# Past keys turned by VectorE and moved by DMA, a new order of the attention turn, and the causal mask added by a matmul

## The reference, cut to what matters

```python
z = einsum('bqhd,bkhd->bhqk', q, k) * HD_B ** -0.5 + bias      # 16 heads, 64 wide
mask = arange(Lk)[None, :] < (q_offset + arange(Lq))[:, None]
u = where(mask, log_sigmoid(-z), 0.0)
rev_excl = cumsum(u, axis=3, reverse=True) - u
A = where(mask, exp(log_sigmoid(z) + rev_excl), 0.0)
out = einsum('bhqk,bkhd->bqhd', A, v)
```

## Time and profile before

| | |
|---|---|
| median of 3 runs | 1518.87 us (1518.58 to 1518.95) |
| the profiled execution's own time | 1517.85 us |
| its span | 1516.1 us |
| attention stage, first projection slice to the last pair's end | 793.8 to 1098.9 us of the span |
| one steady turn | 35.6 us, of which PE busy 31.46, DVE 23.00, ACT 18.62 |
| DMA in the steady turn | 164 GB/s, mean busy share 0.51 |

### The profile page before, as it was taken

One profiled execution on the slowest core, in us unless ns is written; L12 is line 12 of the kernel. 1 busy time (PEld: TensorE's weight loads), 2 busy tenths in 40 slices (PEclk: granted clock), 3 DMA queues, 4 the chain that ended last, 5 costly groups with the idle time before them and its releaser, 6 DMA issues.

```text
span 1516.1 us, 33061 instructions
## 1 busy us (share of the span) xinstructions
PE 1463.3 (97%) x13048; PEld 1391.0 (92%) x13048; DVE 1140.3 (75%) x1855; ACT 776.6 (51%) x1192; POOL 320.0 (21%) x307
## 2 busy tenths in 40 slices
PE   8999999999999999999998888888899999999998
PEld 8999999989999999999997777777699999999998
DVE  7866666668998989889726666666679989899753
ACT  6544444436754636455514555554557546364543
POOL 3000000002322323223141111111243223223221
PEclk9999999999999999999999999999999999999999
DMA  5133333223787786876426554553247777877721
GB/s 189 57 87 86 86 86 86 86 87 93 154 175 166 159 182 149 170 168 147 125 84 210 169 175 162 169 167 112 72 105 153 171 170 157 172 160 163 171 84 63
DMA packets 237716, 205.83 MB, mean 136 GB/s; under 512 B 8268, under 2 KB 224404, under 8 KB 237588
## 3 DMA queue, kind: packets, MB, share of 16 engines
q1 hardware_dynamic: 151346, 147.34, 30.9%
q0 software_dynamic: 68160, 47.20, 20.0%
q10 hardware_dynamic: 18082, 9.48, 2.3%
HBM read 192.19 MB, written 11.80 MB: 135 GB/s over the span
## 4 chain that ended last, share of the span: by engine, by line
PE 88%; DVE 5%; issue 4%; ACT 2%; DVEq 0%; DMA 0%; ACTq 0%
PE acc L2771 21%; PE acc L3095 19%; PE pMO L3095 12%; PE pL L3095 12%; PE acc L3195 5%; PE acc L3032 2%; PE pL L2892 1%; PE acc L3302 1%; PE pMO L3262 1%; PE acc L3318 1%; PE pMO L2961 1%; PE acc L3483 1%; PE acc L3291 1%; DVE pg L2544 1%; PE pMO L3249 1%
## 5 line engine op out<-in xcount | busy, mean ns | idle before, releaser
L654 POOL TENSOR_TENSOR wlo<-wraw,whi 128x512 fp32r<-128x512 f32 x40 | 56.2, 1433 | 455.2 <-ACT whi L768 455.2
L2771 PE MATMUL acc<-xa_hi,whi 128*128 128x288 f32 x544 | 125.2, 311 | 0.6 <-issue 0.6
L854 ACT ACTIVATE hi<-wraw 128x1024 fp32r<-128x1024 f32 x60 | 63.7, 1062 | 106.5 <-DVE wraw L1976 106.2
L2771 PE MATMUL acc<-xa_hi,wlo 128*128 128x288 f32 x544 | 116.6, 296 | 0.0
L837 ACT ACTIVATE hi<-wraw 128x1024 fp32r<-128x1024 f32 x60 | 63.7, 1061 | 102.8 <-PE acc L3095 102.6
L2771 PE MATMUL acc<-xa_lo,whi 128*128 128x288 f32 x544 | 116.2, 295 | 0.0
L3095 PE MATMUL acc<-X_lo,hi 128*128 128x288 f32 x384 | 113.4, 295 | 0.0
L3095 PE MATMUL acc<-X_hi,lo 128*128 128x288 f32 x384 | 113.4, 295 | 0.0
L3095 PE MATMUL acc<-X_hi,hi 128*128 128x288 f32 x384 | 113.2, 295 | 0.0
L1991 DVE TENSOR_TENSOR lo<-wraw,hi 128x1024 fp32r<-128x1024 f32 x60 | 73.4, 1223 | 41.9 <-ACT hi L837 41.9
L3095 PE MATMUL acc<-H_hi,hi 128*128 128x288 f32 x336 | 99.4, 296 | 1.3 <-DVE lo L1997 1.3
(11 more groups left out here) (513 smaller groups left out, 4943.8 us busy)
## 6 DMA issues: line engine op xcount, KB each, us to landing
wraw<-in_w_up_dram SPq DMA_DIRECT2D x64, 512.0 KB, 6.8
wraw<-in_w_down_dram SPq DMA_DIRECT2D x64, 512.0 KB, 6.2
Kp<-in_cache_k_dram SPq DMA_DIRECT2D x32, 512.0 KB, 4.0
Vp<-in_cache_v_dram SPq DMA_DIRECT2D x32, 512.0 KB, 5.6
wraw<-in_w_in_a_dram SPq DMA_DIRECT2D x30, 512.0 KB, 5.1
wraw<-in_w_up_dram POOLq DMA_DIRECT2D x32, 256.0 KB, 4.9
S_even<-in_w_up_dram POOLq DMA_DIRECT2D x32, 256.0 KB, 7.0
S_odd<-in_w_up_dram POOLq DMA_DIRECT2D x32, 256.0 KB, 8.1
```

The costliest lines, as they stand in the source:

```text
L654: ins = pool.tensor_tensor(wlo[s][:, k:k + 2, :], wraw[s][:, k:k + 2, :], whi[s][:, k:k + 2, :].bitcast(F32), ALU.subtract)
L854: act.activation(blocks4(hi31), by_depth(G % 2)[:, 0], ACT.Copy).then_inc(piece_hi, 1)
L2771: last = pe.matmul(acc[a][:, hf, 0:HALF], w[s][:, k, a * P:(a + 1) * P], x[k][:, hf * HALF:(hf + 1) * HALF], start=(k == 0 and n == 0), st ...
```

## The change

- **Keys.** `t_fill` and both `t_copy` are gone. A new `keys_turned(s, g)` on VectorE turns one page (128x1024) within 32x32 blocks into a new buffer `KX`, which holds two pages. A new `keys_moved(s, h)` on SP brings the blocks to their places in `KT` with 16 DMAs per half, each from 32 partitions to 32 partitions, 2 KB a partition. `key_page(s, g)` now waits for `keys_turned` of the page that had the buffer. The turning runs one sequence further ahead (j+2 in turn j).
- **Mask.** `mask` is gone. `logits` has two more matmuls for each query block, identity by mask matrix, both held as float32r, in the same PSUM accumulation; `gates` waits for `z_full`.
- **Banks.** `values_transposed` writes to `TB`; `weights_transposed` alternates between `pM` and `TB`; `new_sums` and `new_values` use `pO`; `fg` shrinks to one group.
- **Order.** All streams have a new order in the turn; SP's loop is written out.

```diff
+            def keys_moved(s, h):
+
+                sp.wait_ge(k_turned, 4 * s + 2 * h + 2)
+                wait(sp, zS_full, 2 * s + h)
+                for a in range(4):
+                    for b in range(4):
+                        sp.dma_start(KT[32 * b:32 * b + 32, a], KX[32 * a:32 * a + 32, b]).then_inc(k_moved, 16)
             def pages_and_weights(j, weights, more_pages):
-                kv_store(j)
-                key_page(j + 1, 2)
-                key_page(j + 1, 3)
-                value_pages(j + 1)
                 if more_pages:
                     key_page(j + 2, 0)
                     key_page(j + 2, 1)
+                kv_store(j)
+                keys_moved(j + 1, 1)
+                value_pages(j + 1)
                 if weights:
                     weights(0)
+                if more_pages:
+                    keys_moved(j + 2, 0)
+                    key_page(j + 2, 2)
+                    key_page(j + 2, 3)
+                if weights:
                     weights(1)
...
+            def keys_turned(s, g):
+
+                dve.wait_ge(kp_landed[g % 2], 32 * s + 16 * (g // 2) + 16)
+                if g % 2 == 0:
+                    wait(dve, k_moved, N_MOVE * (2 * s + g // 2))
+                dve.transpose(KX[:, :, :, g % 2, :].rearrange("p b j k -> p j b k"),
+                              Kp[:, g % 2, :].rearrange("p (j b k) -> p j b k", b=4, k=32)).then_inc(k_turned, 1)
...
+                        if m == 0:
+                            for hh in range(2):
+                                pe.matmul(pL[:, hh, c0 + w - P:c0 + w], ident_r[:], neg_r[:], start=False, stop=False)
```

VectorE's turn from `weights(j, 1, 1)` on is now (`more` is false in the seventh turn only):

```diff
+                new_out(j)
+                for hh in range(2):
+                    products(j, 2, hh)
+                for hh in range(2):
+                    weights(j, 2, hh)
                 past_products(j + 1)
                 past_weights(j + 1)
+                if more:
+                    queries(j + 2)
+                    keys_turned(j + 2, 0)
+                    keys_turned(j + 2, 1)
+                k_low(j + 1)
                 q_low(j + 1)
+                if more:
+                    keys_turned(j + 2, 2)
+                    keys_turned(j + 2, 3)
                 past_out_even(j + 1)
                 past_out_odd(j + 1)
+                kv_copy(j + 1, 1)
```

More of the change, by code:

```diff
@@ L582, in _ @@
             sp.wait_ge(unit_done, U_OB)
+            keys_moved(0, 0)
             value_pages(0)
+            keys_moved(0, 1)
             key_page(1, 0)
             key_page(1, 1)
+            keys_moved(1, 0)
+            key_page(1, 2)
+            key_page(1, 3)
             for a in range(2):
@@ L588, in _ @@
             pages_and_weights(0, lambda a: kv_weights(3, a), True)
-            with sp.Fori(1, NPAIR - 3) as j:
+            for j in range(1, NPAIR - 3):
                 pages_and_weights(j, lambda a: kv_weights(j + 3, a), True)
@@ L2552, in weights @@
                 dve.tensor_tensor(sg[:, hh, cols], sg[:, hh, cols], pg[:, hh, 0:GW[g]], ALU.mult).then_inc(a_done, 1)
-            def group(j, g):
-                for hh in range(2):
-                    products(j, g, hh)
-                for hh in range(2):
-                    weights(j, g, hh)
-            def t_copy(s, f):
-                dve.wait_ge(T_full, 8 * s + f + 1)
-                wait(dve, zS_full, 2 * s + f // 4)
-                dve.tensor_copy(KT[:, 4 * (f % 2):4 * (f % 2) + 4, (f // 2) % 2, :], pO[:].rearrange("p (j k) -> p j k", k=P)
-                                ).then_inc(Td_free, 1)
             def past_products(s):
@@ L2593, in past_store, with pair @@
                                     ).then_inc(fin_free, 1)
-            def pair(j, first):
+            def pair(j, first, more):
                 if first:
@@ L2599, in pair @@
                 k_rows(j)
-                mask(j, 0)
+                products(j, 0, 0)
+                new_rows(j)
+                new_mask(j)
+                if not first:
+                    past_store(j)
+                products(j, 0, 1)
+                weights(j, 0, 0)
                 if first:
@@ L2636, in last_pair @@
                 k_rows(j)
-                mask(j, 0)
+                products(j, 0, 0)
                 new_rows(j)
                 new_mask(j)
-                group(j, 0)
                 past_store(j)
-                mask(j, 1)
+                products(j, 0, 1)
+                ob_low(2)
+                weights(j, 0, 0)
+                weights(j, 0, 1)
                 new_products(j)
-                ob_low(2)
-                group(j, 1)
-                mask(j, 2)
                 ob_low(3)
+                products(j, 1, 0)
+                products(j, 1, 1)
+                for hh in range(2):
+                    weights(j, 1, hh)
+                ob_low(4)
                 new_out(j)
-                group(j, 2)
-                ob_low(4)
+                for hh in range(2):
+                    products(j, 2, hh)
+                for hh in range(2):
+                    weights(j, 2, hh)
                 dve.wait_ge(fin_free, 2 * NSEQ)
@@ L2674, in _ @@
             dve.memset(pN[:, SMP:SMP + 1], 1.0)
-            t_copy(0, 3)
             dve.wait_ge(qb_zero, 1)
             queries(0)
-            t_copy(0, 5)
-            t_copy(0, 7)
+            keys_turned(0, 2)
+            keys_turned(0, 3)
             kv_copy(0, 0)
+            keys_turned(1, 0)
+            keys_turned(1, 1)
+            dve.wait_ge(row_chain, 3)
+            queries(1)
             past_products(0)
@@ L3248, in weights_transposed @@
                     hh, c0 = (b % 2, GCOL[b // 2] + t * P) if b < 4 else (t // 2, GCOL[2] + t % 2 * P)
[L3249 removed]
+                    last = pe.transpose(ABANK[b][:, t * P:(t + 1) * P], sg[:, hh, c0:c0 + P], ident[:])
                 last.then_inc(at_full, 1)
             def weighted(j):
[L3254 removed]
+                pe.wait_ge(n_dve, 6 * j + 6)
                 pe.wait_ge(at_free, N_AT * j + N_AT)
```

248 lines of the change are left out of this document (103 added, 145 removed).

## The result

The changed kernel takes 1635.91 us (median of 4 runs, 1633.90 to 1637.66) against 1518.72 us before on the same chip: ratio 1.0772, 95% interval 1.0753 to 1.0791, slower. The forecast was 1551 us with a range of 1492 to 1588. The direction was right, the size was not: +117 us against +32.

The account below looks back on a forecast made before the run. TensorE's stream bounds the 35.6 us turn; after the change a serial loop of 37.8 plus 1.6 for the clock. Six turns +23, prologue +3, first +7, last -1.5: +32 on 1517.85, plus 1.0 for the median, 1551; range 1492 to 1588.

Parts of the forecast that it names:

- The step that failed: On SP's queue, each keys_moved DMA was taken at 0.40 us to issue, so 6.4 us for a half's 16.
- The loop: Attention stage, one second past_logits to the next: serial moves, pages, turnings and TensorE work sum to 37.8 us a turn.
- The clock: TensorE's wait of 6.5 us halves its clock every turn, with 3.3 us of work at half speed: 1.6 us a turn.
- Prologue and first turn: Before and in the attention stage's first turn, waits for moved keys cost +3 us and +7 us.
- The turning: On VectorE, each keys_turned of a 128x1024 page takes 1.22 us, four a turn, 4.9 us.
- the rival with double turning: On VectorE, float32 elements pass twice, 2.29 us a turning: +30 us, 1581 us; chance 0.11.
- the tie: In the loop, turning at 0.78 and moves at 0.36 us give 34.7 us a turn: 1510 to 1525 us; chance 0.10.
- The mask: On TensorE, eight mask matmuls of 128 columns a turn at 0.13 us each add 1.0 us.
- Landing: A half's moves land in KT 2.0 us after the last issue.
- Transposes taken away: TensorE loses eight t_fill, 3.5 us a turn; with shorter waits and added mask, about 30 us if nothing else ended it.
- The rival of fast moves: On SP, moves issue at 0.20 us each, loop 31.4 us: -29 us, 1489 us; chance 0.22.

Follow-up runs that it names:

- e1: Changed kernel with each half's bytes moved in 4 DMAs of 128 partitions instead of 16 of 32, past keys' output undefined: 1540.3 us.
- e2: Changed kernel with each half's bytes moved in 8 DMAs of 64 partitions instead of 16 of 32, past keys' output undefined: 1564.4 us.
- e3: Changed kernel with SP issuing key pages 2 and 3 ahead of the first half's 16 moves: 1610.3 us.
- e7: Changed kernel with third and fourth turnings in the next turn, key pages ahead of the moves, and half of each batch issued by ScalarE: 1548.7 us.
- e8: Kernel before with only the causal mask changed, two matmuls per diagonal block replacing VectorE's three additions: 1523.6 us.
- e12: Changed kernel with turnings, pages, past logits and prologue reordered, ScalarE issuing 4 of 16 moves, value pages earlier, new_values later: 1505.8 us, 0.9914 of the kernel before.
- e13: e12 with the causal mask added by VectorE again instead of by matmuls: 1519.0 us, ratio 1.0000 to the kernel before.

## Why the prediction was wrong, and where it was right

**The step that failed** is "for 32 partitions I take 0.40, nearer the small one. So a half takes 16 x 0.40 = 6.4 us to issue". It is 0.63 from start to start, 10.05 for a half. The bounds, 0.36 and 0.56, did not hold it either. The nearest row was the upper one, a small store issued behind another (562 ns median, 598 at most), and it was read too low. Its eight issues are of two kinds, four directly behind another issue and four behind a register load, and the median lies between them (kernel before, one of each, with the issue ahead of it):

```profile
824.40 0.55 SPq L546 DMA_DIRECT2D out_dram<-kvn  x1
825.00 0.59 SPq L548 DMA_DIRECT2D out_dram<-kvn  x1
...
896.57 0.53 SPq L548 DMA_DIRECT2D out_dram<-kvn  x1
```

The directly following ones took 588 to 598 ns, and with the gap of 0.04, which the lower bound got and the upper did not, that is the 0.63 of the moves. I leaned to the lower bound, because rows and partitions seemed to be the price, and e1 and e2 show that between 32 and 128 partitions they have none. Why pages and the 4 KB loads are issued in 0.33 to 0.36 us is not shown by any run. With 32 moves in the loop the term is 32 x 0.227 = 7.3 us a turn too small; put into the prediction's own sum it gives 37.8 + 7.3 = 45.1 before the clock. Over six turns that is 44 us; with the 11 us of the prologue and the first turn (below) it makes 55 of the 85 us by which 1551 was short. By this estimate the one term is enough to leave the range: 1551 + 55 = 1606.

**The loop, term by term**, from one second past_logits (966.43) to the next (1016.99), predicted in brackets: past logits and new values 3.3 (1.9), group 2 1.8 (1.9), past scans 1.9 (1.9), queries and two turnings 3.0 (2.8), 16 moves and key page 14.5 (10.8), third and fourth turning 4.2 (2.3), past_out 0.9 (0.8), TensorE to the first past_logits 8.3 (5.7), and from there 1.2, 10.05 and 1.4 (9.6). The sum is 50.6 (37.8; the entries as printed add to 37.7). The chain of causes was named correctly, link by link: the waits stand where it puts them, and e3 to e7, which each loosened one link or two, moved the time. The moves' issues carry 7.3 of the 12.8 us that were missing, and the pages 1.7, for the fourth turning waits for its own page as well. Most of the rest is in the two stretches of TensorE's work behind its waits, where the clock was low; how it divides between clock and mask is not separated.

**The clock.** Taken at 1.6 us a turn. In the loop, past logits and new values took 1.4 and TensorE's stretch 2.6 more than summed, 4.0 together, of which the mask is a part. The wait was 11.6 us and not 6.5, the second one 4.9 and not 2 to 3, and the prediction priced the clock behind the first alone; in the turn before, the 0.50 lasted from the end of the wait, 946, until 950 us. The Trainium skill (TensorE: Matmul & The Clock Gate, "HAM oscillation") has this pattern, a slow start behind every long wait; the trace agrees in each steady turn, where the second past_logits takes 1.93 or 1.94 us in place of 1.07 (mean clock 0.80 in the loop).

**Prologue and first turn.** Taken at +3 and +7; +13.7 and +13.9 measured. Batches in series with pages are in both, and TensorE waited 21.1 us for moved keys in three of its first four past logits. Three batches hold 48 issues, 11 us by the pitch alone, of the 17.6 us that were missing here.

**The turning**: 1.22 taken, 1.233 measured; the rival with double turning is out, and so is the tie. **The mask**: 0.13 us a matmul taken, 0.18 from start to start in e8 (0.22 by busy time); that its net price is the 1.0 us a turn of the sum is luck, since shorter waits, which the sum did not have, gave the difference back. **Landing** 2.0 taken, 2.0 measured, but counted from the start of the issue: behind the end of the last one only 1.4 are left, and the sum had 0.6 too much there. **Transposes taken away**: the prize of "about 30 us" a turn was there; e12 has 32.1, with other edits beside.

**The rival of fast moves** had the case wrong and its rule about right. No move was issued faster. The rule was that the turn has to come under about 34.5 us, since the prologue and the first turn have to be paid too: e13 ties with turns of 33.8 on average, e12 is faster with 32.1, and it got there by taking issues out of the chain.

Where the 117 us went: six steady turns at 50.8 to 51.9 in place of 35.6 make 93, the prologue 14, the first turn 14; the last turn gives back some 4.

## What to carry to other kernels

Count DMA issues in series, not bytes: here one issue occupied its queue for 0.6 us whether it moved 64 or 256 KB, so that a batch of 16 acts like one instruction of 10 us. Price it from single rows of DMAs that directly follow another, not from a median over mixed ones, and where such rows disagree (0.36 and 0.59 us in the kernel before) let the range reach the dearer one with its gap. Take the whole batch as a wait for everything that stands behind it, on this queue and on the engines that wait for it, into the next turn. Before an idea is dropped for such a wait, look whether the batch can start earlier, be shared with a second queue, or be read later: the same operations in another order, with a quarter of the moves on ScalarE's queue, went from 7.7% slower to 0.9% faster.

## What was not expected of the hardware

- A DMA within the chip's SBUF took its queue 591 ns (32 partitions, 64 KB), 597 (64 partitions) and 602 (128 partitions, 256 KB), median; 333 ns was the row of a page from memory behind a register load. The dear figure was in the kernel before, too, in small stores directly behind another issue.
- SP's and ScalarE's queues issued at the same time with 0.63 to 0.67 us an issue each, against 0.63 alone, so the cost is hardly shared.
- Turning a 128x1024 float32 page in 32x32 blocks takes VectorE 1.23 us, as much as the two-input operation of that width.
- Moves took 3.2 us to land from SP's queue and 4.6 from ScalarE's in e12 (medians), with the DMA engines at 0.81 of their time in a turn, and 2.0 in the changed kernel at 0.54.
